# The late two thirds of an adaLN modulation: from TensorE products in the middle of the kernel to row sums on VectorE during the input projection

## The reference

```
mod = silu(c) @ ada_w + ada_b              # c (2, 1024), ada_w (1024, 6144)
sh_a, sc_a, gt_a, sh_f, sc_f, gt_f = split(mod, 6)
h = rms_norm(x, g0) * (1 + sc_a) + sh_a
x = x + gt_a * rms_norm(mixer(h), g1)      # mixer: input projection, attention and RWKV heads, output projection
h = rms_norm(x, g2) * (1 + sc_f) + sh_f
x = x + gt_f * rms_norm(swiglu(h), g3)
```

## Time and profile before

| | us |
|---|---|
| median of three runs (lowest, highest) | 2254.7 (2254.15, 2259.59) |
| the profiled execution | 2253.61 |
| its span | 2251.7 |
| TensorE busy in the span | 1923.4 (85%) |
| VectorE busy | 928.0 (41%) |
| ScalarE busy | 637.8 (28%) |

### The profile page before, as it was taken

One profiled execution on the slowest core, in us unless ns is written; L12 is line 12 of the kernel. 1 busy time (PEld: TensorE's weight loads), 2 busy tenths in 40 slices (PEclk: granted clock), 3 DMA queues, 4 the chain that ended last, 5 costly groups with the idle time before them and its releaser, 6 DMA issues. The chain is left out here.

```text
span 2251.7 us, 41181 instructions
## 1 busy us (share of the span) xinstructions
PE 1923.4 (85%) x17018; PEld 1690.4 (75%) x17018; DVE 928.0 (41%) x1438; ACT 637.8 (28%) x1269; POOL 207.2 (9%) x287
## 2 busy tenths in 40 slices
PE   4999974288899998898842995999999999999996
PEld 3999952156666766666621983999999999999995
DVE  4222254544454445445419119242334233423347
ACT  5322342033334424434324124212111211111114
POOL 0000000022332322423200000100000000000000
PEclk8999997589999999999976998999999999999998
DMA  7111025610100101000092303111011101110122
GB/s 277 47 37 47 28 61 153 201 52 30 35 18 30 35 19 46 19 18 21 16 351 85 132 22 108 38 57 48 25 42 57 47 20 48 56 48 19 47 108 80
DMA packets 112180, 147.85 MB, mean 66 GB/s; under 512 B 65968, under 2 KB 80944, under 8 KB 111568
## 3 DMA queue, kind: packets, MB, share of 16 engines
q1 hardware_dynamic: 112016, 145.41, 19.8%
HBM read 114.90 MB, written 30.50 MB: 65 GB/s over the span
## 5 line engine op out<-in xcount | busy, mean ns | idle before, releaser
L391 PE MATMUL ps<-hhi,whi 128*128 128x364 f32 (+1 forms) x1728 | 573.9, 332 | 74.0 <-DVE wlo L384 38.1
L391 PE MATMUL ps<-hlo,whi 128*128 128x364 f32 (+1 forms) x1728 | 573.4, 332 | 4.7 <-issue 4.7
L391 PE MATMUL ps<-hhi,wlo 128*128 128x364 f32 (+1 forms) x1728 | 572.9, 332 | 0.0
L391 PEld LDWEIGHTS ps<-hhi,whi 128*128 128x128 f32 x1728 | 329.3, 191 | 75.6 <-issue 58.5
L391 PEld LDWEIGHTS ps<-hhi,wlo 128*128 128x128 f32 x1728 | 329.3, 191 | 5.2 <-issue 5.2
L391 PEld LDWEIGHTS ps<-hlo,whi 128*128 128x128 f32 x1728 | 329.3, 191 | 0.0
L384 DVE TENSOR_TENSOR wlo<-wraw,whi 128x1024 fp32r<-128x1024 f32 x74 | 90.5, 1224 | 505.3 <-ACT whi L380 503.4
L727 POOL TENSOR_TENSOR nlev<-gm,con 64x256 f32<-64x256 f32 x204 | 156.3, 766 | 246.0 <-DVE gm L1323 232.0
L1565 DVE TENSOR_TENSOR acc<-acc,ps 128x364 f32<-128x364 f32 (+1 forms) x240 | 126.5, 531 | 101.9 <-PE ps L1982 101.9
L1982 PE MATMUL ps<-ahi,dhi 128*128 128x364 f32 (+1 forms) x480 | 158.5, 330 | 2.4 <-DVE acc L1565 2.4
L1982 PE MATMUL ps<-alo,dhi 128*128 128x364 f32 (+1 forms) x480 | 157.5, 328 | 0.0
(11 more groups left out here) (214 smaller groups left out, 2514.8 us busy)
## 6 DMA issues: line engine op xcount, KB each, us to landing
wraw<-in_w_tiles SPq DMA_DIRECT2D x72, 512.0 KB, 3.5
late<-in_ada_w SPq DMA_DIRECT2D x8, 2048.0 KB, 9.3
ci<-scan SPq DMA_DIRECT2D x17, 768.0 KB, 4.5
draw<-in_w_down SPq DMA_DIRECT2D x20, 512.0 KB, 3.4
slab<-in_ada_w SPq DMA_DIRECT2D x4, 2048.0 KB, 19.0
scan<-mix SPq DMA_DIRECT2D x12, 512.0 KB, 4.4
x<-in_x_t SPq DMA_DIRECT2D x4, 1456.0 KB, 9.5
x<-x_mid SPq DMA_DIRECT2D x1, 4352.0 KB, 13.3
```

Of the source, the lines that this page charges most:

```text
L391: mm = nc.tensor.matmul(ps[:, 3 * u + c, 0:n], w[u][:, k, :], x[:, k, a:a + n], start=(k == 0 and w is whi and x is hhi), stop=(k == KD - ...
```

## The change

The weights of the late two thirds are given to the kernel turned (`ada_t`, 4096 rows of 1024), so that each of 32 tiles of 128 rows, 512 KB, has one output of the modulation on each partition. The conditioning rows are loaded to all 128 partitions (`cond`), and ScalarE takes their Silu there. VectorE then makes, for each tile and each of the two sequences, one instruction that multiplies the tile with the conditioning row and keeps the sum over the row (`accum_out`); the product itself goes to PSUM banks 6 and 7 and isn't read. These instructions stand behind the weight splits of the input projection, three tiles behind each of the first four and two behind each of the next ten (`LATE_SPLITS`). The tiles, two buffers, and one conditioning row lie in rows 9 to 11 of `mix`, which ScalarE fills only after `late_step` says that all sums are done. Bias and the three gains follow on VectorE. The slabs, their products, turns and evictions go from the late stage, and three loops are partly written out.

```diff
-EARLY, SLABS = 4, 12
+EARLY, LATE = 4, 32
+LATE_SPLITS = [3] * 4 + [2] * 10
...
+            for s in range(2):
+                sp.dma_start(cond[s][:, :], d["c_rows"][s:s + 1, :].broadcast_to([P, D])).then_inc(cond_in, 16)
+
+            def load_late(t):
+                if t >= 2:
+                    sp.wait_ge(late_step, 2 * (t - 1))
+                sp.dma_start(late[t % 2][:, :], d["ada_t"][P * t:P * t + P, :]).then_inc(late_in[t % 2], 16)
+
+            for u in range(2):
+                load_weight(sp, 1, u)
+            load_late(0)
+            load_late(1)
+            loaded = 2
+            for i in range(2 * (OUT_M - 2)):
+                load_weight(sp, 2 + i // 2, i % 2)
+                ahead = min(LATE, sum(LATE_SPLITS[:i + 1]) + 2)
+                for t in range(loaded, ahead):
+                    load_late(t)
+                loaded = ahead
...
-            load_slab(EARLY)
             for u in range(2):
                 sp.wait_ge(y_sent[u], 16 * (CHUNKS // 2 + 1 - u) + 16)
...
-            load_slab(EARLY + 1)
             sp.dma_start(bon[:, :, :], d["bonus_rows"].rearrange("j p t -> p j t")).then_inc(bg_back, 16)
...
-            for n in range(EARLY + 2, SLABS):
-                sp.wait_ge(slab_mm, n - 1)
-                load_slab(n)
...
+            act.wait_ge(cond_in, 32)
+            for s in range(2):
+                nc.scalar.activation(cond[s][:, :], cond[s][:, :], ACT.Silu).then_inc(cond_ready, 1)
...
+            for i in range(3, RW_TILES // 2 - 2):
+                for u in range(2):
+                    if 2 * i + 2 + u == 9:
+                        act.wait_ge(late_step, 2 * LATE)
                     raw_rows(i + RM + 1, 2 * i + 2 + u, u)
                     split_hi(act, i + RM + 2, u)
...
+            dve.wait_ge(cond_ready, 2)
+            def late_modulation(count):
+                for t in itertools.islice(late_tiles, count):
+                    dve.wait_ge(late_in[t % 2], 16 * (t // 2 + 1))
+                    for s in range(2):
+                        if t or s:
+                            dve.wait_ge(late_step, 2 * t + s)
+                        nc.vector.scalar_tensor_tensor(out=ps[:, 6:8, :].rearrange("p a b -> p (a b)"), in0=late[t % 2][:, :], scalar=1.0, in1=cond[s][:, :],
+                                                       op0=ALU.mult, op1=ALU.mult, accum_out=mod[:, 4 * EARLY + t, s:s + 1]).then_inc(late_step, 1)
...
                 split_lo(dve, m + 1, u)
+                late_modulation(LATE_SPLITS[n])
...
                 split_lo(dve, MLA_TILES // 2 + 1, u)
+                late_modulation(LATE_SPLITS[MLA_TILES + u])
                 shift_mix(u, u)
...
+                if i == 3:
+                    dve.wait_ge(late_step, 2 * LATE)
+                    rows = mod[:, 4 * EARLY:4 * EARLY + LATE, :]
+                    nc.vector.tensor_tensor(rows, rows, vec[:, V_ADAB + 4 * EARLY:V_ADAB + 4 * EARLY + LATE].unsqueeze(2).broadcast_to([P, LATE, 2]),
+                                            ALU.add).then_inc(late_mod, 1)
+                    dve.wait_ge(late_mod, 1)
+                    gain(1, 16, 0.0)
+                    gain(2, 32, 1.0)
+                    gain(3, 40, 0.0)
...
-                n = EARLY + j
-                ada(n, late[n % 2], late_in[n % 2], 4)
-                if j:
-                    turn_row(n - 1, late_row, 6)
-            pe.wait_ge(mrow_ready, EARLY + KR)
...
-                n = EARLY + KR + j
-                ada(n, late[n % 2], late_in[n % 2], 0)
-                turn_row(n - 1, late_row, 6)
-            turn_row(SLABS - 1, late_row, 6)
```

More of the change, by code:

```diff
@@ L8 @@
+import itertools
 from contextlib import ExitStack, contextmanager
@@ L213, in build @@
         assert end <= END
+        cr0, l0, l1, ends = place(-(-(end - 5 * TM * 4) // 32) * 32, ("cond0", [P, D]), ("late0", [P, D]), ("late1", [P, D]))
+        assert ends <= end - 2 * TM * 4
+        cr1, end = place(end, ("cond1", [P, D]))
+        assert end <= END
+        cond, late = [cr0, cr1], [l0, l1]
         RAW_AT = R2 + (KQ + KKV) * T * 4
@@ L257, in build @@
         assert end <= OATT_AT
-        yn, ysq0, ysq1, LATE_AT = place(R1, ("yn", [P, KR, T]), ("ysq0", [P, T]), ("ysq1", [P, T]))
+        yn, ysq0, ysq1, end = place(R1, ("yn", [P, KR, T]), ("ysq0", [P, T]), ("ysq1", [P, T]))
         ysq = [ysq0, ysq1]
-        l0, l1, r0, r1, end = place(LATE_AT, ("late0", [P, KD, 512]), ("late1", [P, KD, 512]), ("mrow2", [P, P]), ("mrow3", [P, P]))
-        late, late_row = [l0, l1], [r0, r1]
         assert end <= R2
@@ L298, in build @@
         slab_mm, mod_done = sem("slab_mm"), sem("mod_done")
+        cond_in, cond_ready, late_step, late_mod = sem("cond_in"), sem("cond_ready"), sem("late_step"), sem("late_mod")
         gains_done = sem("gains_done")
@@ L525, in _ @@
             load_weight(sp, 0, 1, first=True)
-            with sp.Fori(1, OUT_M) as m:
-                for u in range(2):
-                    load_weight(sp, m, u)
+            for s in range(2):
[15 more added lines that the diff above has]
+                loaded = ahead
             sp.wait_ge(raw_ready, RW_TILES)
@@ L744, in _ @@
                 slot_pool(x, x % 2)
-            pool.wait_ge(o_ev, JOBS * PAIRS + 1)
-            for u in range(2):
-                nc.gpsimd.memset(late_row[u][:, :], 0.0).then_inc(mrow_zero, 1)
             pool.wait_ge(hi_ready, 12)
@@ L766, in put_row @@
                     act.wait_ge(turned, n - 1)
-                act.wait_ge(mrow_zero, 2 if n < EARLY else 4)
+                act.wait_ge(mrow_zero, 2)
                 for j in range(4):
@@ L867, in _ @@
                 split_hi(act, RM + 1, u)
-            with step.loop(RW_TILES // 2 - 2, 6) as i:
+            with step.loop(3, 6) as i:
                 for u in range(2):
+                    raw_rows(i + RM + 1, 2 * i + 2 + u, u)
+                    split_hi(act, i + RM + 2, u)
+            for i in range(3, RW_TILES // 2 - 2):
+                for u in range(2):
+                    if 2 * i + 2 + u == 9:
+                        act.wait_ge(late_step, 2 * LATE)
                     raw_rows(i + RM + 1, 2 * i + 2 + u, u)
@@ L1063, in _ @@
                     y_squares(j)
-                put_row(EARLY + j, late_row, 4)
-                if j:
-                    modulation(EARLY + j - 1, 6)
             for j in range(KR):
@@ L1075, in _ @@
                     y_squares(j + 2)
-                put_row(EARLY + KR + j, late_row, 0)
-                modulation(EARLY + KR + j - 1, 6)
-            modulation(SLABS - 1, 6)
             for j in range(KR):
@@ L1225, in _ @@
             rest(x1, 2, 2)
+            dve.wait_ge(cond_ready, 2)
+            late_tiles = iter(range(LATE))
+            def late_modulation(count):
[6 more added lines that the diff above has]
+                                                       op0=ALU.mult, op1=ALU.mult, accum_out=mod[:, 4 * EARLY + t, s:s + 1]).then_inc(late_step, 1)
             for n in range(MLA_TILES):
@@ L1248, in _ @@
                 split_lo(dve, MLA_TILES // 2 + 1, u)
+                late_modulation(LATE_SPLITS[MLA_TILES + u])
                 shift_mix(u, u)
-            with dve.Fori(0, RW_TILES // 2 - 2) as i:
+            for i in range(RW_TILES // 2 - 2):
                 for u in range(2):
                     split_lo(dve, i + MLA_TILES // 2 + 2, u)
+                    late_modulation(LATE_SPLITS[MLA_TILES + 2 + 2 * i + u] if i < 3 else 0)
                     shift_mix(2 * i + 2 + u, u)
+                if i == 3:
[7 more added lines that the diff above has]
+                    gain(3, 40, 0.0)
             for u in range(2):
@@ L1485, in _ @@
                 nc.vector.tensor_tensor(yt[:, j, :], yt[:, j, :], gat[:, j, :], ALU.mult).then_inc(rw_done, 1)
[L1488 to L1491, removed]
             dve.wait_ge(o_ev, JOBS * PAIRS + 1)
@@ L1626, in ada @@
             def ada(n, source, filled, bank):
-                pe.wait_ge(filled, 16 * ((n - EARLY) // 2 + 1 if n >= EARLY else 1))
+                pe.wait_ge(filled, 16)
                 if n % EARLY >= 2:
@@ L2103 @@
         "x_t": np.concatenate([x["x_prompt"][0], x["x_sample"][0]]).T,
-        "ada_w": x["ada_w"][0],
+        "ada_w": x["ada_w"][0][:, :512 * EARLY],
+        "ada_t": x["ada_w"][0][:, 512 * EARLY:].T,
+        "c_rows": np.concatenate([x["c_prompt"], x["c_sample"]]),
         "w_tiles": w_tiles,
```

3 lines of the change are left out of this document (removed).

## The result

| | before | changed |
|---|---|---|
| median of 4 runs, us | 2254.43 (2251.66 to 2259.59) | 2222.12 (2220.57 to 2223.33) |
| ratio, 95% interval | 1 | 0.9854 [0.9842, 0.9866] |
| profiled execution, us | 2253.61 | 2222.09 |
| its span, us | 2251.7 | 2220.3 |

The change gains 32.3 us by the medians and 31.5 by the two profiled executions. The forecast was 26.7 us, 2228; 2222.12 is at the lower edge of the range, and by the ratio (0.9854 of 2254.7 is 2221.8) a little under it. The forecast's 26.7 us were found almost as worked out, at the output projection's start. Another 5.6 us came behind it, where the prediction had expected nothing. One execution of pad45 and one of double_sums, further down, ran at 2354 and 2367 us with a granted clock of 0.81, and their medians and ratios leave these out.

What follows compares the result with a forecast made beforehand. TensorE's standstill in the late stage, waiting for y rows and weight slabs, was taken as the bound. Input projection 0, y rows -5.5, chain -21.2: 2253.61 - 26.7 = 2226.9, as a median 2228 us; range 2222 to 2240.

Steps and rivals of the forecast that it cites:

- The y rows' term: Late stage: with no slab ahead on the queue, the y rows come back 5.5 us earlier, bounds 0 and 5.8.
- four issues set the end by themselves: Late stage: lower bound 0 for the y rows' gain, if issuing four transfers (12.16 us) alone sets their end.
- The chain's 16.8 us: Late stage: y rows' return through four means to VectorE's first reciprocal takes 16.8 us, clock high after row 0.
- The doubt on the clock: Late-stage means: pauses might keep TensorE at 1.2 GHz, costing 0 to 7.2 us; 0.9 was taken.
- The prediction's own sign of being wrong: Late-stage means: among the listed signs of a wrong prediction, a granted clock of 0.50 (1.2 GHz) there.
- rival A: Late stage: TensorE stays at 1.2 GHz through the means, 7.2 us instead of 0.9, 2234 us; chance 0.15.
- The input projection's term: Input projection: 64 row sums at 1.45 us, 93 us of VectorE's time, fit beside its work; cost 0.
- its formula: Input projection: TensorE's standstill is 64 times the sum's time plus 33.2 minus 170.3 us; none below 2.14 us a sum.
- B: Input projection: row sums run at half rate, TensorE stands still 15.9 us, 2244 us; chance 0.06.
- C: Input projection: half rate plus awaited read-out, 2.7 us a sum, TensorE waits 35.7 us, 2264 us; chance 0.03.
- So a gain before 1181.10 comes out in full: From the first reciprocal (1181.10) to the output projection, 57.56 us stay untouched, so earlier gains reach the total whole.

Runs made afterwards that it cites:

- pad45: Changed kernel with 45 small unused fp32 products on TensorE ahead of the output projection, moving the feed-forward loop's code: 2222.5 us, 0.9852.
- double_sums: Changed kernel with every row sum in the input projection made twice into the same place: 2248.3 us, 0.9965.
- slab_ahead: Changed kernel with an unused 2 MB load in the queue just ahead of the y rows: 2224.5 us.
- no_late_slabs: Kernel before without the loads of its third to eighth late slab, products, turns and evictions kept (wrong weights): 2241.3 us, 0.9926.
- pad14: Changed kernel with 14 small unused fp32 products on TensorE ahead of the output projection: 2209.5 us, 0.9791.
- pad128: Changed kernel with 128 small unused fp32 products on TensorE ahead of the output projection: 2218.1 us, 0.9828.
- pad270: Changed kernel with 270 small unused fp32 products on TensorE ahead of the output projection: 2267.6 us, 1.0047.
- ff_written_out: Changed kernel with the four rounds of TensorE's feed-forward loop written out, so no jump back: 2207.9 us, 0.9783.
- warm_out: Changed kernel with 7 unused fp32 products of 364 columns on TensorE just ahead of the output projection: 2219.0 us.
- pad11: Changed kernel with 11 small unused fp32 products, putting the feed-forward loop's code where the kernel before has it: 2230.7 us, 0.9899.

## Why the prediction was right, and where it failed

- The reason was right: the late stage was held up by the y rows and by slabs (slab_ahead 5.4 us, no_late_slabs 16), and all of it comes out at the output projection, which starts 25.85 us earlier, against 26.7.
- The y rows' term, 5.5, measured 5.38. Of its bounds, 0 (four issues set the end by themselves) is refuted: with the slab gone the issue itself shrank from 12.16 to 6.87 us.
- The chain's 16.8 us with a high clock behind row 0 is right. The doubt on the clock was sized at half a pass (0.9) and cost 1.65, since a second mean ran at the low clock. The prediction's own sign of being wrong, a granted clock of 0.50 during the means, came true for two of the four: rival A in part, at a small share of its 7.2 us. Over seven profiled executions without added warm products the chain is 18.4 (changed, pad14, pad128, pad270, pad45, ff_written_out, warm_out) and in three, with the same code around it, 16.3 to 16.5 (slab_ahead, double_sums, pad11). Whether the clock rises by the second or the third mean isn't settled by anything the runs varied.
- The input projection's term, 0, is right, and so is its formula (double_sums). Rivals B and C fell at once: 1.36 us a sum.
- What failed is a step in the sum: "So a gain before 1181.10 comes out in full", with 0 for everything behind. Up to the output projection it holds. Behind it, the removed 1068 instructions moved TensorE's feed-forward loop against the blocks in which its code is fetched. The stretch with the jumps got 7.1 us shorter (782.9 to 775.8): 5.3 of standstills and 1.8 of low clock behind them. The output projection, the norms and the first 50 us of the feed-forward stage got 1.5 us longer (212.6 to 214.1), most of it in the norms, where more products ran at the low clock (groups of 16 products took 8.19 and 6.54 us where before has 6.81 and 6.83; the others 5.1 in both); no run varied that. Together 5.6. pad11 shows that it is the position: with eleven idle products it brings the second standstill back, 4 products behind the first. By the medians the change gains 32.3 us, and at equal code position 23.6 and 25.8, so the forecast of 26.7 fits the change without the loop's shift. The standstills were in the profile of before, in the chain; the prediction used nothing of it behind the output projection's start, though what a shift of the loop would do to them no row of before shows.

## What to carry to other kernels

Look for "issue" in the chain at a loop's jump back, before pricing any change of an engine's code: adding or removing instructions ahead of a loop of about 1800 on TensorE was worth from -21 to +9 us here, as much as the change itself. Here such a loop was cheap when it ended 17 or 18 instructions into the eighth block from its start, and equally cheap written out, where its position no longer matters for a jump. When a change's gain is checked, compare at equal code position, or stage by stage.

## What was not expected of the hardware

- A jump back of 1805 instructions costs nothing (47.90 us for the next 288 products) or a standstill of 2.4 to 3.0 us, or that and 1.3 to 2.0 us more, by the loop's place among blocks of 256 instructions, and 0.3 to 3.1 us of low clock behind it. The instruction queue has nine packets more for each such jump (129 against 102, 133 against 106).
- The Trainium skill, in "Runtime: NRT & Kernel Launch", section "Instruction fetch mechanics", gives TensorE a first-in first-out store of 2048 instructions refilled in blocks of 256. The runs agree with both: 256 instructions a packet, and no fetch in the kernels whose loop ends early in its eighth block. But to lie in eight blocks isn't enough, as the changed kernel (217 instructions into the eighth) and pad45 (141) are fetched again. The same section says that a taken branch stalls if its target is outside the current two pages. For TensorE the runs differ: a target seven blocks back cost nothing in pad14.
- A row sum on VectorE with two fp32 operands in SBUF takes 1.23 us for 1024 elements, no more than the operation without a sum (1.28, worked out from the earlier trace rows), with the read-out at 0.14. The rule of half throughput in the Trainium skill, "Vector Engine (DVE) Microarchitecture Reference", section "Points that are easy to get wrong", does not hold for it.
- The issue of four DMAs of small pieces took 12.1 to 12.5 us behind a slab of 2 MB (four kernels), 6.8 to 7.4 without it (nine), and 8.1 to 8.2 without it but with products on TensorE meanwhile (three). So the time to issue is no fixed cost; it depends on what else is under way.
